# Order of the first loads, transposes and low halves at the head of a two-block transformer kernel

## What is computed

```python
def rmsnorm(x, g):
    xf = x.astype(jnp.float32)
    y = xf * lax.rsqrt(jnp.mean(xf * xf, axis=-1, keepdims=True) + EPS)
    return (y * g.astype(jnp.float32)).astype(x.dtype)

    h = x
    for l in range(DEPTH):
        n = rmsnorm(h, attn_norm[l])
        proj = n @ w_in[l]
        u, v_sgu, q, k, v_att = jnp.split(
            proj, [D_SGU, 2 * D_SGU, 2 * D_SGU + D_ATTN, 2 * D_SGU + 2 * D_ATTN], axis=-1)
        u = jax.nn.gelu(u)
        v_sgu = jax.nn.gelu(v_sgu)
```

## Time and profile before

| | |
|---|---|
| median of three executions | 1999.46 us |
| the three | 1990.83, 2000.87, 1999.46 us |
| the profiled execution | 1992.1 us, of it 1990.0 from the first instruction to the last |
| TensorE busy | 94% of the span |
| DVE, ScalarE, GpSimd busy | 51%, 39%, 44% |
| mean granted TensorE clock | 0.956 of full speed |

### The profile page before, as it was taken

How to read it: one execution, slowest core, us unless ns; L and a number is a source line. 1 busy time by engine, 2 the same in 40 slices (tenths; PEclk the granted TensorE clock), 3 DMA queues, 4 the chain that set the end, 5 groups by cost and what they waited for, 6 DMA issues and landing times. The chain is left out here.

```text
span 1990.0 us, 26010 instructions
## 1 busy us (share of the span) xinstructions
PE 1872.8 (94%) x8878; PEld 1513.5 (76%) x8878; DVE 1021.1 (51%) x1797; ACT 777.2 (39%) x1235; POOL 882.1 (44%) x1158
## 2 busy tenths in 40 slices
PE   6999999999999999999999999997887799999997
PEld 5767788888887866788888878886555588888885
DVE  6667556666654377566666555333763342222223
ACT  3444443333334344443333334554653242222223
POOL 5543445555555532454555553337001325555551
PEclk9999999999998999999999999988887879999998
DMA  6221224444322221233444321213001202322311
GB/s 232 85 85 43 75 80 145 146 143 147 131 73 97 87 83 43 87 104 136 149 137 148 105 84 66 85 43 127 1 1 43 85 0 95 116 84 86 125 42 43
DMA packets 102964, 183.46 MB, mean 92 GB/s; under 512 B 6714, under 2 KB 66668, under 8 KB 100844
## 3 DMA queue, kind: packets, MB, share of 16 engines
q1 hardware_dynamic: 102504, 181.74, 26.6%
q10 hardware_dynamic: 388, 0.79, 0.1%
HBM read 180.42 MB, written 2.10 MB: 92 GB/s over the span
## 5 line engine op out<-in xcount | busy, mean ns | idle before, releaser
L772 POOL TENSOR_TENSOR w_lo<-raw,w_hi 128x256 fp32r<-128x256 f32 (+1 forms) x1148 | 879.2, 799 | 1068.7 <-ACT w_hi L815 1068.4
L1896 PE MATMUL ps<-n_hi,w_hi 128*128 128x512 f32 x1408 | 560.9, 398 | 9.5 <-DVE n_lo L1278 5.5
L1897 PE MATMUL ps<-n_lo,w_hi 128*128 128x512 f32 x1408 | 551.8, 392 | 0.0
L1898 PE MATMUL ps<-n_hi,w_lo 128*128 128x512 f32 x1408 | 551.5, 392 | 0.0
L815 ACT ACTIVATE w_hi<-raw 128x1024 fp32r<-128x1024 f32 (+1 forms) x331 | 310.5, 944 | 322.6 <-PE ps L1898 199.3
L1896 PEld LDWEIGHTS ps<-n_hi,w_hi 128*128 128x128 f32 x1408 | 266.7, 189 | 70.3 <-issue 9.7
L1897 PEld LDWEIGHTS ps<-n_lo,w_hi 128*128 128x128 f32 x1408 | 266.4, 189 | 57.5 <-issue 3.4
L1898 PEld LDWEIGHTS ps<-n_hi,w_lo 128*128 128x128 f32 x1408 | 266.3, 189 | 56.4
L1896 PE MATMUL ps<-x_hi,w_hi 128*128 128x512 f32 x672 | 273.2, 406 | 8.9 <-DVE x_lo L1278 8.9
L1897 PE MATMUL ps<-x_lo,w_hi 128*128 128x512 f32 x672 | 269.1, 400 | 0.0
L1898 PE MATMUL ps<-x_hi,w_lo 128*128 128x512 f32 x672 | 268.8, 400 | 0.0
(11 more groups left out here) (270 smaller groups left out, 1992.2 us busy)
## 6 DMA issues: line engine op xcount, KB each, us to landing
raw<-in_w_up SPq DMA_DIRECT2D x44, 1024.0 KB, 6.9
raw<-in_w_ff SPq DMA_DIRECT2D x32, 1024.0 KB, 6.1
raw<-in_w_in SPq DMA_DIRECT2D x28, 1024.0 KB, 7.3
zb<-in_ada_w SPq DMA_DIRECT2D x16, 1536.0 KB, 8.1
raw<-in_w_down SPq DMA_DIRECT2D x44, 512.0 KB, 4.3
raw<-in_w_out SPq DMA_DIRECT2D x12, 1024.0 KB, 6.7
za<-in_x SPq DMA_DIRECT2D x1, 2048.0 KB, 10.1
raw<-in_cmp_w_k SPq DMA_DIRECT2D x2, 1024.0 KB, 6.7
```

What stands on the lines that cost most here:

```text
L772: last = pool.tensor_tensor(parts[0][:, c], parts[1][:, c], parts[2][:, c], ALU.subtract)
L1896: pe.matmul(out, l_hi, r_hi, start=start, stop=False)
L1897: pe.matmul(out, l_hi, r_lo, start=False, stop=False)
L1898: return pe.matmul(out, l_lo, r_hi, start=False, stop=stop)
```

## The change

- SP first sends a quarter of stripe vs (feature tiles 0 and 1, 512 KB), then x in four transfers of 512 KB, one for each token tile, with a semaphore each, then the other three quarters of vs, each in a transfer of its own; the first two quarters have semaphores of their own. ScalarE's `hi` waits for quarter 0, quarter 1, or the rest.
- TensorE turns x token tile by token tile as each lands: seven transposes for feature tiles 0 to 6 each time; feature tile 7 comes last, with four. Bank 7 is used for the gains of the norm before it.
- ScalarE's queue brings only the 16 rows of `attn_norm`. These are turned alone (`cols0`, ahead of the last token tile), and DVE copies them before h. The other 15 small transfers move to SP's queue, after the first stripe. All rows together are turned once more as `cols0_rest` in bank 4, after quarter 2 of vs; DVE copies them between `keep_factor` and `angles`, and `tables` on ScalarE waits for that.
- DVE writes the low half of tile f - 1 behind the copy of tile f, instead of all low halves after all copies.

```diff
@@ bank_plan
+    b.take("cols0", 7)
     for f in range(DT):
         b.take(("x", f), f)
-    b.take("cols0", 0)
...
+        if l == 0:
+            b.take("cols0_rest", 4)
@@ sync
-            sp.dma_start(xin, a["x"].rearrange("b (t p) c -> p (b t) c", p=P)).then_inc(x_in, 16)
+            def load_first(q, done):
+                r = raw[0][:, :].rearrange("p (k c) -> p k c", k=DT)
+                v = a["w_in"][0][:, 512:1024].rearrange("(k p) c -> p k c", p=P)
+                sp.dma_start(r[:, 2 * q:2 * q + 2], v[:, 2 * q:2 * q + 2]).then_inc(done, 16)
+
+            load_first(0, first_in[0])
+            for t in range(NT):
+                sp.dma_start(xin[:, t, :], a["x"][0, t * P:(t + 1) * P, :]).then_inc(x_in[t], 16)
+            load_first(1, first_in[1])
+            load_first(2, landed[0])
+            load_first(3, landed[0])
+            for name, (at, k) in ROWS0.items():
+                if name != "attn_norm":
+                    sp.dma_start(rows[0][at:at + k, :], row_view(name)).then_inc(gains_in, 16)
@@ scalar
-            for name, (at, k) in ROWS0.items():
...
-                act.dma_start(rows[0][at:at + k, :], v).then_inc(gains_in, 16)
+            act.dma_start(rows[0][0:DEPTH * DT, :], row_view("attn_norm")).then_inc(gain_in, 16)
...
-                if q == 0:
+                if isinstance(landed_at, list):
+                    act.wait_ge(*landed_at)
+                elif q == 0:
                     act.wait_ge(landed[st.index % 2], landed_at)
...
-                    hi(g, landed_value(by_quarter[g][0]), g - 3 if g >= 4 else None)
+                    first = [first_in[g], 16] if g < 2 else [landed[0], 32]
+                    hi(g, first if g < 3 else landed_value(by_quarter[g][0]), g - 3 if g >= 4 else None)
...
             def tables():
 
+                emptied(act, "cols0_rest")
@@ vector
+            dve.tensor_copy(cols[:, 0, 0:DEPTH * DT], filled(dve, "cols0")[:, 0:DEPTH * DT]).then_inc(freed("cols0"), 1)
+            emptied(dve, "cols0")
             for f in range(DT):
-                if f == HT:
-                    dve.tensor_copy(cols[:, 0, 0:NROWS0], filled(dve, "cols0")[:, 0:NROWS0])\
-                        .then_inc(freed("cols0"), 1)
                 dve.tensor_copy(h[:, f, :], filled(dve, ("x", f))[:, :]).then_inc(free[f], 1)
-            emptied(dve, "cols0")
+                if f >= 1:
+                    emptied(dve, ("x", f - 1))
+                    raw_lo(("attn", 0), f - 1)
+            emptied(dve, ("x", DT - 1))
+            raw_lo(("attn", 0), DT - 1)
...
-            for f in range(DT):
-                emptied(dve, ("x", f))
-                raw_lo(("attn", 0), f)
             for f in range(DT):
                 add_square(("attn", 0), f)
             for l in range(DEPTH):
                 keep_factor(("attn", l))
                 if l == 0:
+                    c = slice(DEPTH * DT, NROWS0)
+                    dve.tensor_copy(cols[:, 0, c], filled(dve, "cols0_rest")[:, c]).then_inc(freed("cols0_rest"), 1)
+                    emptied(dve, "cols0_rest")
                     angles()
@@ tensor
-            pe.wait_ge(x_in, 16)
-            for f in range(DT):
-                out = bank(("x", f))
-                for t in range(NT):
-                    last = pe.transpose(out[:, t * P:(t + 1) * P], xin[:, t, f * P:(f + 1) * P], ident)
-                last.then_inc(full[f], 1)
...
+            outs = [bank(("x", f)) for f in range(DT - 1)]
+            for t in range(NT):
+                if t == NT - 1:
+                    k = DEPTH * DT
+                    pe.wait_ge(gain_in, 16)
+                    pe.transpose(bank("cols0")[:, 0:k], rows[0][0:k, :], ident[0:k, 0:k])\
                         .then_inc(full[BK["cols0"][0]], 1)
+                pe.wait_ge(x_in[t], 16)
+                for f in range(DT - 1):
+                    last = pe.transpose(outs[f][:, t * P:(t + 1) * P], xin[:, t, f * P:(f + 1) * P], ident)
+                    if t == NT - 1:
+                        last.then_inc(full[f], 1)
+            out = bank(("x", DT - 1))
+            for t in range(NT):
+                last = pe.transpose(out[:, t * P:(t + 1) * P], xin[:, t, D - P:D], ident)
+            last.then_inc(full[DT - 1], 1)
...
+                    if l == 0 and (q, t) == (2, NT - 1):
+                        pe.wait_ge(gains_in, 16 * (len(ROWS0) - 1))
+                        pe.transpose(bank("cols0_rest")[:, 0:NROWS0], rows[0][0:NROWS0, :], ident[0:NROWS0, 0:NROWS0])\
+                            .then_inc(full[BK["cols0_rest"][0]], 1)
```

More of the change, by code:

```diff
@@ L467, in build @@
         ada_in, ada_used = sem("ada_in"), sem("ada_used")
-        consts_in, x_in, pos_in = sem("consts_in"), sem("x_in"), sem("pos_in")
-        gains_in, rows_in = sem("gains_in"), sem("rows_in")
+        consts_in, pos_in = sem("consts_in"), sem("pos_in")
+        x_in = [sem(f"x_in{t}") for t in range(NT)]
+        first_in = [sem(f"first_in{q}") for q in range(2)]
+        gain_in, gains_in, rows_in = sem("gain_in"), sem("gains_in"), sem("rows_in")
         lam_in, sguw_in, sgub_in, cw2_in = sem("lam_in"), sem("sguw_in"), sem("sgub_in"), sem("cw2_in")
@@ L592, in landed_value, with row_view @@
             return 32 * (st.index // 2 + 1)
+        def row_view(name):
+            v = a[name]
+            if len(v.shape) == 1:
+                return v.rearrange("(r p) -> r p", p=P)
+            if len(v.shape) == 2:
+                return v.rearrange("l (r p) -> (l r) p", p=P)
+            return v.rearrange("l w (r p) -> (l w r) p", p=P)
         block = ctx.enter_context(nc.Block())
@@ L678, in load_ada @@
                 sp.dma_start(ada_w, a["ada_w_2"][0][bass.ds(k * P, P), l * ADA_W:(l + 1) * ADA_W]).then_inc(ada_in, 16)
-            sp.dma_start(xin, a["x"].rearrange("b (t p) c -> p (b t) c", p=P)).then_inc(x_in, 16)
+            def load_first(q, done):
[11 more added lines that the diff above has]
+                    sp.dma_start(rows[0][at:at + k, :], row_view(name)).then_inc(gains_in, 16)
             for l in range(DEPTH):
                 for j, name in ((1, "vs"), (0, "u"), (4, "va")):
-                    load_f((name, l), a["w_in"][l][:, j * 512:(j + 1) * 512])
+                    if (name, l) != ("vs", 0):
+                        load_f((name, l), a["w_in"][l][:, j * 512:(j + 1) * 512])
                     if l == 0 and j == 0:
@@ L2007, in _ @@
             pe.wait_ge(consts_in, 16)
-            pe.wait_ge(x_in, 16)
-            for f in range(DT):
-                out = bank(("x", f))
-                for t in range(NT):
-                    last = pe.transpose(out[:, t * P:(t + 1) * P], xin[:, t, f * P:(f + 1) * P], ident)
-                last.then_inc(full[f], 1)
-                if f == HT - 1:
-                    pe.wait_ge(gains_in, 16 * len(ROWS0))
-                    pe.transpose(bank("cols0")[:, 0:NROWS0], rows[0][0:NROWS0, :], ident[0:NROWS0, 0:NROWS0])\
-                        .then_inc(full[BK["cols0"][0]], 1)
+            outs = [bank(("x", f)) for f in range(DT - 1)]
[4 more added lines that the diff above has]
+                    pe.transpose(bank("cols0")[:, 0:k], rows[0][0:k, :], ident[0:k, 0:k])\
+                        .then_inc(full[BK["cols0"][0]], 1)
+                pe.wait_ge(x_in[t], 16)
[7 more added lines that the diff above has]
+            last.then_inc(full[DT - 1], 1)
             pe.wait_ge(ones_set, 4)
```

## The result

The changed kernel takes 2002.2 us (median of 22 runs), the kernel before 1995.96 us (22 runs on the same chips). The ratio is **1.0025, 95% interval 1.0014 to 1.0036: about 5 us slower** (3 to 7; the two medians lie 6.2 us apart). That is inside the 0.5% bound and inside the range given, but the forecast was a shift of -0.1 us, and the interval excludes it. The profiled execution spans 2000.3 us at a mean clock of 0.952 (before: 1990.0, 0.956).

What follows compares the result with a forecast made beforehand. TensorE, busy 1872.8 of 1990.0 us, was taken as the bound; -5.1 (start) + 1.5 (DVE) + 2.7 (rows) + 0.8 (clock) = -0.1 us, profiled 1992.0. Median forecast 1998.0, nearer the upper group of runs; range 1988.5 to 2003.0.

Steps and rivals of the forecast that it cites:

- Transfers: At the head: a 512 KB quarter ahead of x costs x 1.32 us; x whole at 12.35, tiles landing in turn.
- rival C: At the head: x's four tiles land together at 12.35, x0 at 17.1, chain +2.7 to +3 us; chance 0.06.
- The prediction's other sum: At the head: a fixed cost of about 2.0 us for each of three more transfers puts x at 18.4.
- First product: TensorE's first product at the head: starts at 17.6 instead of 22.75, 5.1 us earlier.
- Norm's sums: After DVE's additions: last ends at 33.2 (31.5 to 34.8), so the norm comes 3.6 us earlier (2.0 to 5.3).
- signs named as speaking against the prediction: Tile 2 of u before 58, no wait on w_lo there, or DVE's low halves at 0.69 us with GpSimd busy.
- TensorE's wait at the norm: Ahead of the norm's sums: TensorE there by 28.6, its wait for DVE growing from 1.32 to about 4.6 us.
- The rest's rows: Between keep_factor and angles(): DVE waits for the cols0_rest transpose, angles() 2.7 us later measured from the norm.
- Clock: Behind the norm's wait: half clock costs up to 1.6 us; half taken, +0.8 us (0 to 1.6).
- the prediction's second sum: Chain to tile 2 of u with the whole clock price due: -0.9 us turns into +0.7.
- rival B: Norm and tile 2 of u: full 1.6 us clock fall at both waits, +2.3 us, median about 2000.3; chance 0.2.
- Queue D: SP's queue: small rows delay the second stripe or late inputs, up to +7 us, median 2005; chance 0.03.

Runs made afterwards that it cites:

- e2: The change with the transpose of cols0_rest moved ahead of the norm's sums, from (2, 3) to (1, 3); ratio 1.0006 to the kernel before.
- e4: The kernel before with only the split of the rows: norm's gains turned alone, all rows again after (2, 3), with the change's waits; ratio 1.0032 to the kernel before.
- e5: The change with twelve unread matmuls ahead of the norm's sums and twelve ahead of tile 2 of u; ratio 1.0018 to the kernel before.
- e9: The change with the edits of e1 and e2, and twelve unread matmuls ahead of the norm's sums only; ratio 1.0002 to the kernel before.
- e7: The change with the edits of e1 and e2, norm's sums moved after (2, 1) and spread after (2, 3); ratio 0.9976 to the kernel before.
- e10: Same code as e7, measured once more for its interval; ratio 0.9976 to the kernel before.
- e1: The change with ScalarE's wait for cols0_rest in tables() moved from ahead of the first Sin to ahead of Abs; ratio 1.0016 to the kernel before.
- e8: e7 with the weight quarters of u's tiles 2 and 3 brought ahead of tables() on ScalarE; ratio 1.0006 to the kernel before.
- e6: The change with the edits of e1 and e2, and DVE's low halves again after all eight copies of h; ratio 0.9991 to the kernel before.
- e3: The change with the edits of both e1 and e2; ratio 0.9993 to the kernel before.
- e11: e7 with x again in one 2 MB transfer behind the first quarter of the weights; ratio 1.0012 to the kernel before.

## Right and wrong, step by step

- **Transfers.** Foretold: tiles of x at 8.4, 9.7, 11.0 and 12.35, one after the other. Measured: TensorE began at 7.79 and was through with tiles 0 to 2 at 12.3. Right, 0.6 us early; rival C, that they land together, did not happen. The prediction's other sum, with x whole at 18.4, is refuted: the last tile was being turned at 12.47.
- **First product.** Foretold 17.6, measured 17.58. **Norm's sums.** Foretold 33.2, measured 33.31. These two agree better than the terms in them, and that is luck. DVE's first copy came at 12.91, 0.6 early. And a low half beside a busy GpSimd did not always cost 1.16: GpSimd was busy from 17.67, and the two low halves at 18.33 and 19.59 took 0.75. This was one of the signs named as speaking against the prediction. The two errors together saved 1.6 us or so (the additions began at 25.08 instead of 26.7), and the additions, all seven at 1.16, took it back: they ran 8.09 us, where I had taken two or three at that price.
- **TensorE's wait at the norm.** Foretold about 4.6 us, measured 2.99. The sum took the 48 matmuls behind the first product at full clock, 11.0 us; they began at 17.58 and the last at 29.93, as seven or eight of them, from 19.09 on, ran at half clock behind TensorE's wait of 3.68 us for the first product. It cost nothing, since TensorE waits for DVE behind them.
- **The rest's rows.** Foretold +2.7 between the norm and angles(). Measured in DVE's rows: 3.23 us from the factor's copy to angles(), 0.72 before, +2.51. Right, and e2 and e4 show it to be the main loss.
- **Clock: the step that failed, by its size.** The sum took +0.8 us at the norm, 1.6 at most, from one half-clock stretch of 3.4 us. Measured from sums to spread: +2.83 (6.57 against 3.74). That is more than the whole price, so the prediction's second sum, with all of the 1.6 and +0.7 us in the end, was nearer and still short. The stretch lasted until about 39.4, all of the norm's sums and ten of the twelve matmuls, so it was longer than the one from which the price had been taken. Filling the wait took exactly this away (e5, e9).
- **Clock at tile 2 of u: missing in the sum.** The wait there was foretold (1.5 to 3 us; measured 3.14), and rival B had priced a fall behind it, but the sum had no term for it. Measured: +1.34 us (from +2.53 at tile 2 to +3.87 at 75.90). This holds for the one execution profiled: e4 had a wait of the same 3.14 us and no fall, e7 and e10, the same kernel, one without and one with a fall behind the same 2.49 us.
- **Sin's table load: missing in the sum and in every rival.** +1.3 us, shown by e1. In part it was masked: the two small products of the lambdas at the start of angles() took 0.49 us instead of 1.04, as GpSimd now stood idle. Together +0.71 us from the start of angles() to tile 2 of u (19.10 against 18.39).
- **Sum again, with what was measured:** -3.52 (norm) + 2.83 (clock) + 2.51 (rows) + 0.71 (table load less the faster start of angles) = +2.53 at tile 2 of u, +1.34 (clock) = +3.87 at va. The sum foretold was -0.1. Of the 4 us between the two, the clock at the norm makes 2.0 (2.83 for 0.8), the clock at tile 2 1.3 and the table load 0.7; the terms for the norm and the rows were within 0.2. Angles() was foretold at about 42 and tile 2 within 2 us of 60.8; they came at 44.20 and 63.30. Another stretch of half clock behind va made it +5.5 us by 130 us, after which it stayed between 4.0 and 5.9 to 1218 us. The timed difference is 5.0.
- **Rivals.** It went nearest to B, slower by the clock at both waits, with 2.83 and 1.34 us where B had 1.6 and 1.6, and with the table load, which no rival had. B was given a chance of 0.2 and +2.3 us. Queue D did no harm: SP issued the second stripe at 10.91, later than before, and ScalarE never waited for it.
- **From the profiled run to the median.** I started from a median of three, 1999.46; over 22 runs the kernel before has 1995.96. The starting point was so 3.5 us too high and the shift some 5 us too small, and the two partly cancel: that the predicted 1998.0 is off by only 4.2 us is luck.

**What stays open.** Why the rest of the kernel takes 772.6 to 785.3 us from run to run: it goes with half-clock stretches after 1200 us (clock 0.85 to 0.89 over 1200 to 1400), but what starts the long ones was not found. Whether the head's start time has a part in that is open too; e5, e8 and e9, whose heads are 0.8 to 5.4 us ahead of the kernel before, don't show it in time. So the repeated gain of e7 is measured, but what carries it to the end, when e9 with a head as early has none, is not shown. Why a wait of the same length sometimes has a half-clock stretch behind it and sometimes none is open as well.

## What to carry to other kernels

An earlier start of the first product is worth only what the next join passes on: here DVE's chain to the norm let through 3.5 of 5.2 us, and the rest went into a wait that put the array at half clock. Price an idle stretch of TensorE at its length plus the slow matmuls behind it, put useful matmuls there (e7, the only version that was faster by time), and let the engine be late rather than idle if the join doesn't move (e6). When a wait is added, look at what the waiting engine would otherwise have run under its old wait, the load of a function table above all.

## What was not expected of the hardware

- A second wait ahead of an activation moved its table load of 1.28 us from 38.61 to 55.05, behind both waits; with the single wait it ran at 35.48 (e1), 20 us ahead of the function. The load was late in the change, e2, e4 and e5, which have the second wait, and early in e1, e3 and e6 to e11, which have not.
- TensorE's clock fell behind waits as short as 1.8 to 3.1 us (e1, e3, the change), and the half-clock stretch then lasted 3.4 or 6.8 us. In e2 a wait of 2.63 us cost 1.3 us between sums and spread, in the change one of 2.99 cost 2.8. In e4 a wait of 3.14 us, in e7 and e11 one of 2.49 and in e1 one of 1.83 ahead of tile 2 had no half clock behind them. A price taken from one stretch was about half of what the change paid at the norm.
- Of DVE and GpSimd on two inputs each at the same time, it isn't always DVE that pays. In the change two low halves, at 18.33 and 19.59, took 0.75 us while GpSimd's four subtractions took 1.02 on average; in e7 the low halves in their place, from 17.95 on, took 1.3 us and GpSimd's 0.91:

```profile
18.33 0.75 DVE L1304 SCALAR_TENSOR_TENSOR n_lo<-h,cols,n_hi 128x512 fp32r<-128x512 f32 x1
```

```profile
L798 POOL TENSOR_TENSOR w_lo<-raw,w_hi 128x256 fp32r<-128x256 f32 x4 | 3.9, 1020 | 5.9 <-ACT w_hi L835 5.9
```

```profile
17.95 1.32 DVE L1304 SCALAR_TENSOR_TENSOR n_lo<-h,cols,n_hi 128x512 fp32r<-128x512 f32 x1
```

```profile
L798 POOL TENSOR_TENSOR w_lo<-raw,w_hi 128x256 fp32r<-128x256 f32 x5 | 4.4, 909 | 5.5 <-ACT w_hi L835 5.5
```

The first two fences are the change, the last two e7: a row of DVE's timeline, then GpSimd's group from 17 to 21.3 us with its busy time and the mean ns of one.
